# Six places for the down weights of the first layer's experts, fetched two experts ahead of gate and up

## The reference, cut to what matters

```python
def moe_ffn(h, router_w, router_bias, w_gate, w_up, w_down, sh_gate, sh_up, sh_down):
    scores = jax.nn.sigmoid(h @ router_w)                       # 64 experts
    _, idx = lax.top_k(scores + router_bias, TOP_K)             # 8 of them for each token
    s_sel = jnp.take_along_axis(scores, idx, axis=-1)
    gates = s_sel / jnp.sum(s_sel, axis=-1, keepdims=True) * ROUTED_SCALE
    ...                                                         # rows sorted by expert
    hid = jax.nn.silu(xb @ w_gate[e]) * (xb @ w_up[e])          # 1024 -> 256, for each expert e
    y = hid @ w_down[e]                                         # 256 -> 1024, times the row's gate
    ...                                                         # summed back by token
    shared = (jax.nn.silu(h @ sh_gate) * (h @ sh_up)) @ sh_down # the shared expert, all tokens
    return routed + shared
```

## Time and profile before

| | us |
|---|---|
| median of 3 runs (1868.5 to 1869.87) | 1868.97 |
| the profiled execution, its own time | 1868.22 |
| its span | 1866.3 |
| first layer's rounds, from the first gate and up to the last down | 452.5 to 1012.4 |

### The profile page before, as it was taken

How to read it: one execution, slowest core, us unless ns; L and a number is a source line. 1 busy time by engine, 2 the same in 40 slices (tenths; PEclk the granted TensorE clock), 3 DMA queues, 4 the chain that set the end, 5 groups by cost and what they waited for, 6 DMA issues and landing times. The chain is left out here.

```text
span 1866.3 us, 23162 instructions
## 1 busy us (share of the span) xinstructions
PE 1662.9 (89%) x8531; PEld 742.8 (40%) x8531; DVE 572.1 (31%) x1352; ACT 314.1 (17%) x688; POOL 209.0 (11%) x197
## 2 busy tenths in 40 slices
PE   5999998999999999999996599788799999979896
PEld 2544444454434343334432244454333333333332
DVE  2041775465222122222211551474421111111112
ACT  2102442130111111111111111271101000100002
POOL 0300442001111111111110000030000000000000
PEclk9999999999999999999999799998899999989999
DMA  9423993036999999999995924002799999999993
GB/s 352 132 87 123 379 369 120 1 136 259 417 395 410 419 416 403 406 408 402 414 415 214 409 109 156 29 1 80 298 418 400 420 418 407 417 420 414 419 405 126
DMA packets 125649, 560.88 MB, mean 301 GB/s; under 512 B 17442, under 2 KB 22961, under 8 KB 75360
## 3 DMA queue, kind: packets, MB, share of 16 engines
q1 hardware_dynamic: 107104, 512.28, 68.5%
q0 software_dynamic: 17248, 43.62, 6.2%
q10 hardware_dynamic: 1184, 3.47, 0.5%
HBM read 550.02 MB, written 26.80 MB: 309 GB/s over the span
## 5 line engine op out<-in xcount | busy, mean ns | idle before, releaser
L1693 PE MATMUL ps<-wb,pool 128*32 128x512 f32 (+2 forms) x2608 | 488.5, 600 | 16.8 <-issue 16.7
L1693 PEld LDWEIGHTS ps<-wb,pool 128*32 128x32 f32 (+2 forms) x2608 | 160.2, 124 | 305.5 <-issue 305.4
L1707 DVE TENSOR_TENSOR ffn_hid<-ffn_sg,ps 128x256 f32<-128x256 f32 x71 | 29.9, 422 | 605.2 <-ACT ffn_sg L1701 605.2
L1737 PE MATMUL ps<-pool,ffn_hidT 128*32 128x512 f32 (+2 forms) x584 | 164.8, 598 | 21.9 <-DVE ffn_hidT L1722 11.5
L1737 PE MATMUL ps<-hT,ffn_hidT 128*32 128x512 f32 (+2 forms) x680 | 156.5, 597 | 19.6 <-DVE ffn_hidT L1722 14.7
L1600 POOL DMA_INDIRECT pool<-h_rows,ffn_index x71 | 75.8, 1068 | 639.8 <-DVE ffn_index L1650 313.4
L2339 PE MATMUL ps<-wb,hT 128*128 128x512 f32 x320 | 140.0, 599 | 1.6 <-issue 1.6
L1701 ACT ACTIVATE ffn_sg<-ps 128x256 f32<-128x256 f32 x71 | 27.3, 384 | 486.0 <-PE ps L1693 486.0
L1737 PE MATMUL ps<-sh_wd,ffn_hidT 128*32 128x512 f32 (+2 forms) x272 | 100.3, 597 | 4.6 <-DVE ffn_hidT L1722 2.6
L1755 PE MATMUL ps<-x_res,rw 128*128 128x512 f32 x224 | 103.1, 603 | 0.9 <-ACT x_res L1783 0.9
L1663 PEld LDWEIGHTS ps<-const,pool 128*128 128x128 f32 x568 | 77.4, 194 | 66.1 <-issue 62.7
(11 more groups left out here) (305 smaller groups left out, 1779.0 us busy)
## 6 DMA issues: line engine op xcount, KB each, us to landing
wb<-in_expert_w_gate_dram SPq DMA_DIRECT2D x108, 1024.0 KB
wb<-in_expert_w_up_dram SPq DMA_DIRECT2D x108, 1024.0 KB
pool<-in_expert_w_down_dram SPq DMA_DIRECT2D x52, 1024.0 KB, 18.4
hT<-in_expert_w_down_dram SPq DMA_DIRECT2D x52, 1024.0 KB, 16.8
wb<-in_ada_w_dram SPq DMA_DIRECT2D x24, 2048.0 KB, 11.4
sh_wd<-in_expert_w_down_dram SPq DMA_DIRECT2D x24, 1024.0 KB, 19.6
mix_yr<-y_rows SPq DMA_DIRECT2D x7, 2048.0 KB, 11.7
wb<-in_diff_w_in_dram SPq DMA_DIRECT2D x6, 2048.0 KB, 16.5
```

What stands on the lines that cost most here:

```text
L1693: mm = nc.tensor.matmul(core.ps[lo:lo + width, gu_bank(n), :], xT[:, n % 2, k, lo:lo + width], w[:, k], start=k == 0, stop=k == KD - 1, sk ...
L1707: nc.vector.tensor_tensor(hid[:, n % 2, :], sg[:, n % 2, :], core.ps[:, gu_bank(n), F:2 * F], ALU.mult).then_inc(hid_ready, 1)
L1737: mm = nc.tensor.matmul(core.ps[lo:lo + width, down_bank(half), :], hidT[:, n % 2, k, lo:lo + width], wd_at(q % DR, half, k), start=k == 0 ...
```

## The change

The first layer gets six places for down weights in place of five. The new place is the second half of `shared_wgu`; it stands fifth, and the shared expert's down weights `sw.wd` become the sixth. It is free when the other places of its kind are, at `sh_gu`. LAG becomes -2 for the first layer, so six downs are fetched ahead of the loop, and in the loop the down of expert q + 2 stands behind the gate and up of expert q. For the second layer LAG stays 1, the downs ahead of the loop stay four, `DR - 1` is 4 and the places are the same.

```diff
-WEIGHT_RINGS = ((4, 5), (6, 5))
+WEIGHT_RINGS = ((4, 6), (6, 5))
@@ feed_forward
     EARLY = GU - 1 if GU > STREAM else GU
-    LAG = EARLY - STREAM
+    LAG = EARLY - DR + (GU > STREAM)
@@
         wd = [core.pool[:, 0, :], core.pool[:, 1, :], core.hT[:, 0:4, :].rearrange("p k t -> p (k t)"),
-              core.hT[:, 4:8, :].rearrange("p k t -> p (k t)"), sw.wd[:].rearrange("p k d -> p (k d)")]
+              core.hT[:, 4:8, :].rearrange("p k t -> p (k t)")]
+        if GU == STREAM:
+
+            wd.append(shared_wgu[:, 2 * D:4 * D])
+        wd.append(sw.wd[:].rearrange("p k d -> p (k d)"))
@@ sp_down
-            elif q < 4:
+            elif q < DR - 1:
 
                 sp.wait_ge(sh_gu, NT)
@@ sync block
                 for q in range(EARLY):
                     sp_gate_up(sp, q)
-                for q in range(STREAM):
+                for q in range(EARLY - LAG):
                     sp_down(sp, q)
```

## The result

The changed kernel takes 1873.81 us (median of 10 runs, 1871.95 to 1875.81) against 1869.73 us of the kernel before (10 runs, 1867.65 to 1872.97): a ratio of 1.0020, 95% interval 1.0012 to 1.0028. That is 2.2 to 5.2 us more. The forecast was 1869.8, a change of +0.8 us, too small to be told from none; the time lies in the range of 1863.5 to 1875, but it moved by five times the forecast's +0.8.

A forecast was written before the change was run, and what follows sets the result against it. TensorE was taken to bound the first layer's rounds, with 8.1 us lost to late gate and up. Terms 0.8 + 0.2 - 0.2 = +0.8 us gave 1869.8 us, range 1863.5 to 1875.

The forecast's parts named there:

- The sixth place buys nothing: First layer's downs: fetching them earlier gains 0, since TensorE waits for gate and up, at most 1.2 us for down.
- A pair lands by the count of MiB ahead of it: First layer's fetch queue: pair q has 3q - 12 MiB ahead before and after, so its landing doesn't move.
- The cover: Double ends (two experts end in one round): a pair's 5.1 us of fetching covers 5.9 us to the down; 0.8 us lost.
- How many places pay it: Double ends without backlog: the first pays +0.8 us, three others +0.2 us of up to 2.4.
- upper bound of +3.2 us: Whole change: the unknown terms' slower end, with all of the 2.4 us at three further double ends paid.
- rival 2: Slower: the new order of waits costs at all 21 double ends, 16.8 us, 1885.8; a third gives 1874.6; chance 0.19.
- rival 3: First layer's queue: a down waits for its place, so the lead isn't had in full; 1869.0; chance 0.63 with the forecast.
- Rival 1: Faster: longer run-ahead smooths late gate and up pairs in the first layer, up to 9.8 us, 1859.2; chance 0.18.
- The first double end: Ahead of round 2: TensorE's wait grows from 0.40 to about 1.2 us; pair 5 goes out at 467.6 us.
- The end: Last rounds, 41 and 42, of the first layer: small hidden waits may vanish, 0 to -0.3 us, taken as -0.2.
- Signs named ahead of time: First layer: gate and up waits 7 to 11 us, downs landing 18.9 us or more after issue, double-end share down up to 0.06.

The follow-up runs named there:

- e4: Changed kernel with six down places but the old fetch order, no lead, four downs ahead of the loop: ratio 1.0004 to the kernel before.
- e3: Changed kernel with six down places but downs only one expert ahead, five downs ahead of the loop: ratio 1.0001 to the kernel before.
- e6: Changed kernel, six down places and lead of two, but each fetch issued as its place comes free: ratio 1.0012 to the kernel before.
- e2: Kernel before, five down places and old order, only the second pair of a double end also waits for the round's down product: ratio 1.0001.
- e5: Kernel before, five down places and old order, the down behind each pair also waits for a down product, holding back the next pair: ratio 1.0020.
- e1: The changed kernel measured again, nothing altered: ratio 1.0022 to the kernel before.
- e8: Kernel before with five down places, downs one expert ahead, five downs ahead of the loop: ratio 1.0019.
- e9: Changed kernel's 14 MiB cut as five pair places and four down places, each fetch issued as its place comes free: ratio 1.0014 to the kernel before.
- e10: Changed kernel's 14 MiB cut as five pair places and four down places, fixed order, down q-1 behind pair q: 1867.46 us, ratio 0.9984 to the kernel before.
- e7: Kernel before with five down places, five downs ahead of the loop, each fetch issued as its place comes free: ratio 1.0011.
- e11: The kernel before profiled a second time, nothing altered: first layer's rounds 559.6 us.

## Why the prediction was right or wrong, point by point

- **The sixth place buys nothing: right.** e4 has the place and no lead, e3 the place and a lead of one: 559.7 and 559.8 us of rounds. By the clock their ratios are 1.0004 and 1.0001. What TensorE waits for, ahead of down, is 1.2 us in the changed kernel as before.
- **A pair lands by the count of MiB ahead of it, so the lead costs nothing by itself: borne out as far as the runs go.** e3 has a lead of one and rounds of 559.8 us; e6 keeps the lead of two, in another order, and has rounds of 560.7 us, though by the clock it is 2 us slower than before. The rule that was weighed (the Trainium skill, DMA: Bandwidth & Descriptors, Rules for kernel authors: issue a DMA early, wait on it late) gave nothing here; the thing issued earlier wasn't waited for, 1.2 us ahead of down before and after.
- **The cover, 5.1 us of fetching against 5.9 us to the down, 0.8 us lost: right in mechanism and size.** The holes measure 0.62 to 0.78 us by their bytes. The prediction put the cause on both the down and the pair behind it; e2 shows that holding back the pair alone costs nothing, since a down in front of the wait makes the cover 3 MiB, and e5 that the wait ahead of the down makes the holes.
- **How many places pay it: wrong, and this is the term that was mis-sized.** The prediction let the first double end pay 0.8 us and took 0.2 of a possible 2.4 for three others. Seven places have a hole, 4.8 us by their bytes, the five shown 3.5 of them, and the rounds are longer by 2.1 to 3.0 us, 3.7 in e5. Two of the seven come behind double ends (rounds 19 and 27) that the prediction didn't list, though the stretch of round 19, from 698.18 to 712.92 us, has a share of 0.95 and 380 GB/s before the change and would have belonged in the earlier trace rows. The argument that an almost dry queue starts a pair right behind its last packets missed the point: the hole isn't ahead of the pair but behind it, and it came behind every double end whose round ended thin. The upper bound of +3.2 us was nearer than +0.8.
- **The rivals.** By its size the outcome is rival 2, which had a chance of 0.19 and the words "with a third of them 1874.6": seven of 21 double ends have a hole, and the time is 1873.81. Its condition, little backlog when the pair goes out, held in those seven and not in the rest, and the median landing of 18.9 us, the argument against it, said nothing of the thin ones. The wait itself is the one that rival 3 described, a down that waits for its place and holds up the queue; rival 3 was wrong in that it cost nothing. Rival 1, a gain, did not come. That the time lies in the range is owed to the part of rival 2 that the range took in.
- **The first double end:** 0.40 to 0.91 us, and 1.6 in e1, against 1.2 predicted. Pair 5 went out 6.7 us after pair 4, against 467.6 - 460.31 = 7.3.
- **The end:** the round from 978.83 us has 0.78 of DMA share against 1.00 in its like before, so the fetches are done earlier. What that saved in the last rounds is not measured apart; 0.3 us was the most that was counted.
- **Signs named ahead of time:** the total of 7 to 11 us of waits was the forecast's sign, and it is 11.9. A down was to land 18.9 us or more after its issue; where the profile of the changed kernel gives a landing (the 20 downs in `hT`) the median is 15.5, against 18.5 for the same places before, so this sign was wrong. The share in the rounds with a double end was to fall by up to 0.06 where it was under 1; it went from 0.91, 0.98, 0.96 and 0.93 to 0.93, 0.97, 0.99 and 0.96, since the hole stands in the round behind. "Pairs behind a double end waited for in rounds that had no wait" was the sign of a wrong cover, and round 22 has such a wait; but e4, which has no wait behind a pair and 422 GB/s at the start of round 20, has one there as well (0.85 us), so it goes with the clock of round 20 and decides nothing.
- **What stays open.** The rounds explain 2.1 to 3.0 us of the 4. In the first profile the second layer's stretch after its projections is at a lower granted clock, and 0.8 us longer, which would be another part:

```profile
1197.50:1267.80 70.30, 53.27 (x308) 35.68 (x309) 49.00 (x117) 43.42 (x128) 18.60 (x16) 0.89 0.01 4
```

against, before,

```profile
1192.50:1262.00 69.50, 55.12 (x309) 35.74 (x310) 49.15 (x117) 43.48 (x128) 18.65 (x16) 0.91 0.01 4
```

for the same work. From the end of the rounds to the second layer's rounds it takes 340.7 to 341.8 us in nine profiles (341.6 before) and 342.8 to 343.0 in four (changed, e5, e8 and e9), all of kernels that are among the slower ones by the clock; but e1 is as slow and has 341.4. Whether the shifted time of the rounds moves this clock step, or it falls by chance, no run here settles.

## What to carry to other kernels

In a queue written in one order, look at what stands directly behind each large fetch. If it waits longer than the fetch takes, and nothing is left of earlier fetches, the engines move less for that long: here at seven of 21 double ends. It costs time where what is fetched behind is soon waited for: that of round 6 cost none, and e10 has five such holes and is still the fastest kernel here. A lead that the places don't fully cover multiplies such waits, 37 in place of 21 here. Before adding a place to a ring, ask whether that ring's item is ever waited for; the same 14 MiB, cut so that the ring that is waited for has the additional place, gained 3 us here in one order of the queue (e10) and lost 3 in another (e9). And look for holes in stretches of 2 us: a stage whose DMA share reads 1.00 in both kernels had seven of some 0.7 us each.

## What the runs showed that was not expected

Holding back a 2 MiB pair by 3.3 us more at the first double end, and likewise at the others, cost nothing measurable (e2, 1.0001; 66.0 us of waits of the queue on a down product against 30.0), while holding back the 1 MiB down in front of it by 4.4 us, and the pair with it, cost as much as the whole change (e5, 1.0020).

And a wait of TensorE of about 2 us at the same place, ahead of round 20, came with a gate and up of 8.78 us in seven profiles (before, e2, e3, e5, e6, e7, e11) and of 7.09 in four (changed, e1, e4, e8). Over its first 2 us the granted clock was 0.63 to 0.78 in the seven, a part of them at 1.2 GHz, and 1.00 in the four. The waits were 1.98 to 2.28 us in the seven and 1.60 to 1.93 in the four. That is 1.7 us of the rounds, nearly as much as the change itself, so the length of a kernel's rounds is read here with the clock of round 20 beside it.
